# Normalisation and shift applied behind the gate and up products in the second and fourth feed-forward

## What is computed

```python
def rms_norm(x, g):
    y = x * lax.rsqrt(jnp.mean(x * x, axis=-1, keepdims=True) + EPS)
    return y * g
def modulate(h, shift, scale):
    return h * (1.0 + scale[:, None, :]) + shift[:, None, :]
def swiglu(h, w_in, w_out):
    g, u = jnp.split(h @ w_in, 2, axis=-1)
    return (jax.nn.silu(g) * u) @ w_out
h = modulate(rms_norm(x, norm_g[layer, 2]), sh, sc)
x = x + 0.5 * (1.0 + g)[:, None, :] * swiglu(h, ffn_w_in[layer, 1], ffn_w_out[layer, 1])
```

## Time and profile before

| | |
|---|---|
| three runs | 1314.81 us median, 1313.96 to 1315.42 |
| the profiled execution | 1313.54 us, of which 1311.8 us are its span |
| mean granted clock of TensorE | 0.994 of 2.4 GHz |
| busy share of the span | PE 96%, DVE 82%, ACT 48%, POOL 14% |
| `ffn1`, first to last matmul of its units | 254.6 to 444.7 us |
| `ffn3`, the same | 770.2 to 960.3 us |

### The profile page before, as it was taken

One profiled execution on the slowest core, in us unless ns is written; L12 is line 12 of the kernel. 1 busy time (PEld: TensorE's weight loads), 2 busy tenths in 40 slices (PEclk: granted clock), 3 DMA queues, 4 the chain that ended last, 5 costly groups with the idle time before them and its releaser, 6 DMA issues.

```text
span 1311.8 us, 26641 instructions
## 1 busy us (share of the span) xinstructions
PE 1258.3 (96%) x10570; PEld 1228.0 (94%) x10570; DVE 1070.9 (82%) x1668; ACT 629.1 (48%) x990; POOL 189.1 (14%) x204
## 2 busy tenths in 40 slices
PE   2999999999999999999999999999999999999996
PEld 1999999899999889999999999999998989999996
DVE  6998978898888777988878778999978588895674
ACT  3543344544344556553346653434354675455453
POOL 5598800000000000000001000000001014530000
PEclk8999999999999999999999999999999999999999
DMA  9998887389888369988953389887655598555461
GB/s 365 385 338 308 297 312 270 131 324 333 310 304 290 120 203 360 334 293 307 310 205 106 115 250 337 296 304 255 222 182 174 113 185 179 171 163 178 175 196 49
DMA packets 110924, 319.73 MB, mean 244 GB/s; under 512 B 24096, under 2 KB 35808, under 8 KB 110560
## 3 DMA queue, kind: packets, MB, share of 16 engines
q1 hardware_dynamic: 110816, 318.23, 72.8%
HBM read 313.18 MB, written 5.01 MB: 243 GB/s over the span
## 4 chain that ended last, share of the span: by engine, by line
PE 88%; DVE 7%; ACT 3%; issue 1%; DMA 1%; SPq 0%; ACTq 0%; DVEq 0%
PE tiles L375 18%; PE tiles L377 18%; PE tiles L376 18%; PE acc L375 8%; PE acc L377 8%; PE acc L376 8%; PE nrm L551 2%; DVE w_lo L367 2%; PE tiles L577 1%; DVE arena L1468 1%; PE tiles L579 1%; PE tiles L594 1%; ACT w_hi L363 1%; DMA x<-in_x_t 1%; DVE arena L1423 1%
## 5 line engine op out<-in xcount | busy, mean ns | idle before, releaser
L363 ACT CAST w_hi<-land 128x1024 fp32r<-128x1024 f32 x391 | 408.4, 1047 | 457.8 <-PE tiles L377 292.1
L367 DVE TENSOR_TENSOR w_lo<-land,w_hi 128x1024 fp32r<-128x1024 f32 x391 | 486.3, 1251 | 146.0 <-ACT w_hi L363 144.7
L375 PE MATMUL tiles<-x_hi,w_hi 128*128 128x256 f32 x1384 | 393.5, 284 | 0.8 <-DVE arena L1868 0.5
L376 PE MATMUL tiles<-x_lo,w_hi 128*128 128x256 f32 x1384 | 391.6, 283 | 0.0
L377 PE MATMUL tiles<-x_hi,w_lo 128*128 128x256 f32 x1384 | 391.6, 283 | 0.0
L375 PEld LDWEIGHTS tiles<-x_hi,w_hi 128*128 128x128 f32 x1384 | 265.5, 192 | 3.0 <-issue 1.0
L376 PEld LDWEIGHTS tiles<-x_lo,w_hi 128*128 128x128 f32 x1384 | 265.6, 192 | 0.1
L377 PEld LDWEIGHTS tiles<-x_hi,w_lo 128*128 128x128 f32 x1384 | 265.6, 192 | 0.0
L1423 DVE SCALAR_TENSOR_TENSOR arena<-arena 128x1024 f32<-128x1024 f32 x184 | 227.3, 1239 | 11.7 <-ACT arena L1157 8.3
L375 PE MATMUL acc<-h_hi,w_hi 128*128 128x256 f32 x704 | 199.3, 283 | 0.0
L376 PE MATMUL acc<-h_lo,w_hi 128*128 128x256 f32 x704 | 199.2, 283 | 0.0
(11 more groups left out here) (338 smaller groups left out, 1599.7 us busy)
## 6 DMA issues: line engine op xcount, KB each, us to landing
land<-in_stream SPq DMA_DIRECT2D x391, 512.0 KB, 4.5
arena<-in_gstream SPq DMA_DIRECT2D x184, 512.0 KB, 6.5
w_dram<-arena SPq DMA_DIRECT2D x3, 512.0 KB, 6.3
arena<-w_dram SPq DMA_DIRECT2D x6, 256.0 KB, 9.6
arena<-in_c_rows SPq DMA_DIRECT2D x2, 512.0 KB, 5.1
x<-in_x_t SPq DMA_DIRECT2D x1, 1024.0 KB, 10.1
arena<-in_ssm_bn SPq DMA_DIRECT2D x1, 1024.0 KB, 8.2
u_dram<-arena SPq DMA_DIRECT2D x1, 1024.0 KB, 5.3
```

Of the source, the lines that this page charges most:

```text
L363: nc.scalar.copy(w_hi[:, u % RING], land[:, u % LAND]).then_inc(hi_done, 1)
L367: nc.vector.tensor_tensor(w_lo[:, u % RING], land[:, u % LAND], w_hi[:, u % RING].bitcast(F32), ALU.subtract).then_inc(lo_done, 1)
L375: nc.tensor.matmul(outs, lh, rh, start=first, stop=False, **kw)
L376: nc.tensor.matmul(outs, lh, rl, start=False, stop=False, **kw)
```

## The change

In `ffn1` and `ffn3` only (`LATE`), the products with `w_in` are taken of x times (1 + scale) times the norm's gain, without 1/rms; 1/rms (`rx_late`) multiplies gate and up results. The shift is two equal columns more (columns 256 and 257) in the moving operand `xs_hi`, `xs_lo`, so the product of weights and shift comes as a column of each result. `tiles`, `nrm` and `av_bank` become four banks of one tensor `quad`, of which gate and up of one hidden tile take one each. The order of units becomes gate j, output j-2, up j. `keep_busy` goes at these two places; the squares are summed in pairs on VectorE and then by four matmuls in place of eight.

```diff
+            def late_unit(bank, u, i):
+                pe.wait_ge(lo_done, i * 12 + (u + 1))
+                m = products(pe, quad[:, bank, 0:T + 2],
+                             [(*w_tile(u, k * P, P), xs_hi[:, k], xs_lo[:, k]) for k in range(KT)])
+                m.then_inc(used, 1)
+            def ffn_late(f, stage):                                   # TensorE
...
+                first_units(base, [quad[:, b, 0:T + 2] for b in range(3)], xs_hi, xs_lo, KT * stage)
+                for k in range(0, KT, 2):
+                    pe.wait_ge(sq_pair, 4 * e + k // 2 + 1)
+                    m = nc.tensor.matmul(late_sum, ones, t_buf[:, k], start=(k == 0), stop=(k == KT - 2))
+                m.then_inc(nrm_done, 1)
+                late_unit(3, base + 3, 0)
...
+                            pe.wait_ge(silu_done, i * 4 + (FFN_TILES * f + j - 1))
+                            late_unit(2 * (j % 2), g_unit(f, j), i)
+                            out_unit(f, j - 2, o_unit(f, j - 2), i, 4)
+                            pe.wait_ge(freed["d"], i * 4 + (nd + j - 1))
+                            late_unit(2 * (j % 2) + 1, u_unit(f, j), i)
...
-            sum_squares(2)
-            keep_busy(7)
-            ffn(1, 2)
+            ffn_late(1, 2)
...
+            def late_rows(stage, n, ready, unit, before=None):        # ScalarE
+                nc.scalar.activation(eps_root, con("eps", 1), ACT.Sqrt)
+                for k in range(KT):
+                    ready(k)
+                    nc.scalar.activation(x_hi[:, k], x[:, k], ACT.Identity,
+                                         scale=coef[:, stage, k:k + 1]).then_inc(xh_done, 1)
+                for k in range(KT):
+                    nc.scalar.square(t_buf[:, k], x[:, k]).then_inc(sq_done, 1)
+                split_hi(act, unit)
...
+                nc.scalar.activation(rx_late, late_sum, ACT.Sqrt, bias=con("eps", 1), scale=1.0 / D).then_inc(rt_done, 1)
+                nc.scalar.activation(eps_root, con("eps", 1), ACT.Silu)
+            def ffn_late(f):                                          # ScalarE, one round
...
+                            split_hi(act, g_unit(f, j), i)
+                            late_shifts(f, j - 2, i, 4)   # copies the two shift values out of PSUM
+                            late_silu(f, j - 2, i, 4)     # silu(gate + shift), waits for scaled_done
+                            split_hi(act, o_unit(f, j - 2), i)
+                            late_hi(f, j - 2, i, 4)       # h_hi, waits for late_hidden
+                            split_hi(act, u_unit(f, j), i)
...
+            def late_scale(f, j, i, per):                             # VectorE
+                V.tensor_tensor(gate_up[:, j % 2], quad[:, b:b + 2, 0:T], rx_late.unsqueeze(1).to_broadcast([P, 2, T]),
+                                ALU.mult).then_inc(scaled_done, 1)
+            def late_hidden(f, j, i, per):
+                V.scalar_tensor_tensor(out=gate_up[:, j % 2, 1], in0=gate_up[:, j % 2, 1],
+                                       scalar=shift_s[:, j % 2, 1:2], in1=gate_up[:, j % 2, 0],
+                                       op0=ALU.add, op1=ALU.mult).then_inc(freed["d"], 1)
+            def late_lo(f, j, i, per):
+                V.tensor_tensor(h_lo[:, j % 2], gate_up[:, j % 2, 1], h_hi[:, j % 2].bitcast(F32),
+                                ALU.subtract).then_inc(h_done, 1)
...
+                for k in range(0, KT, 2):
+                    dve.wait_ge(sq_done, KT * n + k + 2)
+                    V.tensor_tensor(t_buf[:, k], t_buf[:, k], t_buf[:, k + 1], ALU.add).then_inc(sq_pair, 1)
+                split_lo(dve, unit)
+                dve.wait_ge(rt_done, n + 1)
+                link(V.reciprocal(rx_late, rx_late))
...
                             for s in range(3):
                                 split_lo(dve, u + s, i)
+                                if late and s == 0:
+                                    late_scale(f, j - 2, i, 4)
+                                if late and s == 1:
+                                    late_hidden(f, j - 2, i, 4)
+                                if late and s == 2:
+                                    late_lo(f, j - 2, i, 4)
...
+            norm_coef(2)
+            late_shift(2, 0)
+            split_lo(dve, UNIT["ffn1"] + 1)
             for k in range(KT):
                 wait_tile(dve, TILE["pool"] + k)
                 update(k, tiles[:, k % 2, 0:T], 1, freed["d"])
-            split_lo(dve, UNIT["ffn1"] + 1)
-            norm_coef(2)
```

More of the change, by code:

```diff
@@ L129, in att2_tile, with g_unit, u_unit, o_unit @@
     return TILE["att2+zm"] + 2 * g
-def g_unit(base, j):
-    return base + (2 * j if j < 2 else 3 * j - 1)
-def o_unit(base, j):
-    return base + (65 if j == FFN_TILES - 1 else 3 * j + 4)
+LATE = (1, 3)
+LATE_STAGE = {1: 2, 3: 6}
+def g_unit(f, j):
+    return FFN_BASE[f] + (2 * j if j < 2 else 3 * j - (2 if f in LATE else 1))
+def u_unit(f, j):
+    return FFN_BASE[f] + (2 * j + 1 if j < 2 else 3 * j)
+def o_unit(f, j):
+    if f in LATE:
+        return FFN_BASE[f] + (3 * j + 5 if j < FFN_TILES - 2 else 44 + j)
+    return FFN_BASE[f] + (65 if j == FFN_TILES - 1 else 3 * j + 4)
+def rows_before(stage):
+    return KT * sum(n not in LATE_STAGE.values() for n in range(stage))
 def build_program(nc, stream, gstream, c_rows_d, k_tab_d, vecs_d, cons_d, mask2_d, band_d, xin, pos_d, ssm_bw, ssm_bn, ssm_c, out):
@@ L638, in out_unit @@
                     m = products(pe, yT[n], [(*w_tile(u, n * P, P), h_hi[:, j % 2], h_lo[:, j % 2])],
-                                 start=(j == 0 and per == 0 and n % 2 == 0),
+                                 start=(j == 0 and n % 2 == 0),
                                  stop=(j == FFN_TILES - 1 and per == 0), skip_group_check=True)
@@ new lines, in late_hi @@
+            def late_hi(f, j, i, per):
+                nd = OWNER[:TILE[f"ffn{f}"]].count("d")
+                act.wait_ge(freed["d"], i * per + (nd + j + 1))
+                act.wait_ge(used, i * 3 * per + (FFN_BASE[f] + 3 * j))
+                nc.scalar.copy(h_hi[:, j % 2], gate_up[:, j % 2, 1]).then_inc(late_hh, 1)
+            def ffn_late(f):
+                base = FFN_BASE[f]
+                j0 = 2
+                for part, (reps, _) in enumerate(SEGMENTS[f]):
+                    with act.Fori(0, reps) as i:
+                        for m in range(4):
+                            j = j0 + m
+                            split_hi(act, g_unit(f, j), i)
[4 more added lines that the diff above has]
+                            split_hi(act, u_unit(f, j), i)
+                    j0 += 4 * reps
+                split_hi(act, base + 64)
+                late_shifts(f, FFN_TILES - 2, 0, 0)
+                late_silu(f, FFN_TILES - 2, 0, 0)
+                late_hi(f, FFN_TILES - 2, 0, 0)
+                late_shifts(f, FFN_TILES - 1, 0, 0, 0, 1)
+                late_silu(f, FFN_TILES - 1, 0, 0)
+                split_hi(act, base + 65)
+                late_shifts(f, FFN_TILES - 1, 0, 0, 1, 1)
+                late_hi(f, FFN_TILES - 1, 0, 0)
@@ L1430, in hidden @@
             def hidden(f, j, i, per):
-                base, nd = FFN_BASE[f], OWNER[:TILE[f"ffn{f}"]].count("d")
-                J = FFN_TILES * f + j
+                nd = OWNER[:TILE[f"ffn{f}"]].count("d")
+                J, plain = FFN_TILES * f + j, FFN_TILES * sum(n not in LATE for n in range(f)) + j
                 dve.wait_ge(silu_done, i * per + (J + 1))
@@ new lines, in late_rows @@
+            def late_rows(stage, n, e, unit):
+                for k in range(KT):
+                    dve.wait_ge(xh_done, KT * stage + k + 1)
+                    V.scalar_tensor_tensor(out=x_lo[:, k], in0=x[:, k], scalar=coef[:, stage, k:k + 1],
+                                           in1=x_hi[:, k].bitcast(F32), op0=ALU.mult,
+                                           op1=ALU.subtract).then_inc(xl_done, 1)
+                for k in range(0, KT, 2):
[4 more added lines that the diff above has]
+                link(V.reciprocal(rx_late, rx_late))
@@ L1533, in ffn @@
             def ffn(f, stage, pre, gate_col, ahead_units, next_stage):
-                base, b = FFN_BASE[f], G_FFN[f]
-                for s in range(pre, 5):
-                    split_lo(dve, base + s)
-                hidden(f, 0, 0, 0)
+                base, b, late = FFN_BASE[f], G_FFN[f], f in LATE
+                if not late:
+                    for s in range(pre, 5):
+                        split_lo(dve, base + s)
+                    hidden(f, 0, 0, 0)
                 b += G_FIRST[f]
@@ L1560, in ffn @@
                                     out_part(5 * (part - 1) + OUT_AT.index(3 * m + s))
-                            hidden(f, j - 1, i, 4)
+                            if not late:
+                                hidden(f, j - 1, i, 4)
                             if f == 2:
@@ L1568, in ffn @@
                 blocks[0] = b
-                split_lo(dve, o_unit(base, 21))
+                if late:
```

(14 more changed lines are left out.)

133 lines of the change are left out of this document (88 added, 45 removed).

## The result

| | before | after |
|---|---|---|
| runs side by side | 1314.89 us median (1313.96 to 1315.42) | 1345.93 us median (1344.23 to 1346.73) |
| ratio | | 1.0234, 95% interval 1.0222 to 1.0246 |
| the profiled execution, its span | 1313.54, 1311.8 us | 1346.24, 1344.4 us |

The change makes the kernel 31.0 us slower. Where the time goes is read from four marks, which divide each execution into five stretches: the first matmul of each sum of squares that stands in both kernels (L551 before, L573 after; the one at 15 us is left aside), which is where a stage hands over to the next.

A forecast was written before the change was run, and what follows sets the result against it. TensorE was taken as the bound, 88% of the last-ending chain. Terms -7.4 (starts), +10.5 (first stalls), +9.5 (ffn1), +16.3 (ffn3) sum to +28.9 on 1313.54, giving 1342.4; as a median 1343.7 us, range 1328 to 1352.

The forecast's parts named there:

- The round: In late rounds of ffn1 and ffn3, two VectorE-ScalarE hand-overs make a round 9.01 us against TensorE's 8.67.
- The first stalls: At the start of ffn1 and ffn3, TensorE idles 2.55 us, then 2.7 us again; +10.5 us in all.
- Rival 4: At both starts, two pauses of 2.6 us make the clock fall to 1.2 GHz: +3 to +8, some 1349; chance 0.05.
- Ahead of `ffn1`: Before ffn1's rounds, first units start without the root: 5.6 us gained, 2.9 after squares and columns.
- the last tile: At the end of each late feed-forward, the last tile comes late: 0.7 us in ffn1, 0.8 in ffn3.
- `ffn3`'s rounds: In ffn3, hand-overs plus out_part and power_part beside the rounds; with 0.8 for the last tile, +16.3 us.
- The 1334 at the low end: Whole kernel with silu and late_hi at their lower bounds: 10 us less than the forecast.
- Rivals 1 to 3: The first of these: hand-overs in late rounds are quicker, a round stays under 8.67 us; +16, 1331 us; chance 0.12.
- rival 2: In both late feed-forwards TensorE keeps a lead, so the 7.4 us gain remains: 1307 us; chance 0.07, 0.05 of it faster.
- Rival 3: In gate and up products the two columns cost more than in proportion, 13 ns a matmul: about 1350 us; chance 0.05.

The follow-up runs named there:

- Both together: The changed kernel with both splits (output and up unit) moved ahead in ScalarE's order and gate unit 2's halves made ahead of the root: 1306.99 us.
- The first gate unit's halves: The changed kernel with w_hi and w_lo of gate unit 2 made ahead of the wait for root and reciprocal: 1342.57 us.
- both splits ahead: The changed kernel with ScalarE's split of the output unit ahead of silu and that of the up unit ahead of late_hi: 1310.99 us.

## Why the prediction was right

1343.7 us was predicted and 1345.93 measured; by the profiled executions +28.9 and +32.7.

**The round** was the largest term and holds. Predicted from one `w_lo` of a gate unit to the next, with the idle time ahead of the output unit's `w_lo`: 9.01 and 1.6 us; measured 9.06 outside the loop and 1.57. (By the prediction's own steps the idle time is 3.34 - 1.83 = 1.51; its 1.6 does not follow from them.) Ahead of the up unit's: 0.37 and 0.28 (0.36 in the loop). The durations taken from neighbours were scale 0.69 (measured 0.68), silu from SBUF 0.50 (0.51), `late_hidden` 0.48 (0.48), `late_hi` 0.40 (0.41). That the mechanism is this one, moving one split shows: -33.1 us.

**Too small by 2.0 us:** the twelve rounds of `ffn1` that are a loop take 0.13 and the others 0.05 more than 9.01. The term that was too small is the 0.03 us taken for every hand-over between engines: it holds from ScalarE's split to VectorE's `w_lo`, but scale to silu took 0.09 to 0.10 in every round read, and `late_hidden` to `late_hi` took 0.11 in the loop. No row showed it before, when rounds went at TensorE's pace.

**The first stalls** were 2.55 and 2.7. In `ffn1` 2.59 and 2.52. In `ffn3` 2.65 and 1.00: the second is short only because the gate unit before it ran at the lower clock. Products of 258 columns, timeline of TensorE after:

```profile
792.58 0.42 PE L397 MATMUL quad<-xs_hi,w_hi 128*128 128x258 f32 x1
...
795.16 0.42 PE L397 MATMUL quad<-xs_hi,w_hi 128*128 128x258 f32 x1
```

Twelve products in 2.58 us are 0.215 each: the 1.2 GHz level. **Rival 4 came true in part**, and what it said of the fall being partly under the round too: TensorE would have stood for h in any case. The granted clock is 0.50 in four stretches of the changed kernel: the one of these products, and at the start of `ffn1`, inside `ffn3` and in a stage that was not touched:

```profile
269.80:273.20 3.40, 3.21 (x15) 3.24 (x16) 3.40 (x7) 0.00 (x0) 0.00 (x0) 0.50 0.80 270
874.00:877.40 3.40, 3.40 (x18) 3.40 (x18) 2.71 (x5) 1.19 (x2) 0.00 (x0) 0.50 0.89 340
1201.70:1205.00 3.30, 3.30 (x66) 3.30 (x63) 3.30 (x6) 0.38 (x1) 0.00 (x0) 0.50 0.48 164
```

The pauses of TensorE just ahead of the last two:

```profile
873.38 0.35 PE L397 MATMUL acc<-h_hi,w_hi 128*128 128x256 f32 x1 [2.24 <-DVE h_lo L1584]
1200.54 0.33 PE L1055 MATMUL quad<-arena 64*64 64x64 f32 x2 [2.17 <-DVE arena L2110]
```

So it doesn't take the two pauses of the rival. In `ffn1` the clock falls at the second, in `ffn3` already at the first. In the 14 traces, start-up and the last 20 us aside, there are 23 falls, and each starts within 1.6 us of the end of a pause of 2.0 to 2.7 us, none behind a shorter one. Another 11 pauses of that length are followed by no fall, so the same pause can go either way: of 2.17 us at 1200.54 here with a fall, of 2.16 us at the same line in the kernel with both changes ("Both together") without. The price of the falls at the starts is near nothing, not the 3 to 8 us of the rival: in `ffn1` the slow time lies behind the second stall (an output and the up unit) and the silus come 10.20 and 10.21 us apart, as in the kernel without that fall (10.21 and 10.21, "The first gate unit's halves"); in `ffn3` 9.05 and 9.06 in both. The Trainium skill (TensorE: Matmul & The Clock Gate, A second HAM failure mode: psum-queue depth-cycling) tells of a clock that falls and rises with small idle times between groups; the trace agrees only for pauses of 2 us and more. `ffn1`'s rounds from 298 us on, with a short stop of TensorE in each, are granted 1.00.

**Ahead of `ffn1`** I had first units directly behind the last band matmul. They wait for the last update of x:

```profile
247.24 0.38 PE L812 MATMUL quad<-arena 128*128 128x128 f32 x2
248.25 0.36 PE L599 MATMUL quad<-xs_hi,w_hi 128*128 128x258 f32 x1 [0.62 <-DVE x L1653]
```

The first units use the banks that the updates read (`wait_bank` ahead of `first_units`), a wait that I had not followed: 0.6 us.

**Behind both feed-forwards** the next sum of squares comes 0.9 us later after the last output product than before: 1.13 us of wait, 0.23 at both places of the kernel before. Timeline of ScalarE after:

```profile
453.88 0.41 ACT L1160 CAST h_hi<-arena 128x256 fp32r<-128x256 f32 x1 [2.09 <-DVE arena L1577]
454.19 2.95 ACT L385 CAST w_hi<-land 128x1024 fp32r<-128x1024 f32 x3
457.16 1.28 ACT L1102 ACT_TABLE_LOAD   x1
```

`late_hi` of the last tile waits 2.09 us with three splits and the table load queued behind it. I had costed the last tile up to TensorE's output unit (0.7 and 0.8; measured 0.77 and 0.86) and not what stands behind it in ScalarE's queue. In the kernel with both splits ahead the wait is 0.74 us.

**`ffn3`'s rounds** were laid out at 188.9 us for twenty (20 x 8.67 + 15.5) and took 190.6.

**The rest:** +0.8, not looked for: a wait for the transfer of `ssm_bw` (0.7 us, none before) and later waits of attention products. **What I left out altogether** is TensorE's pace, -2.7 us in the two untouched stretches. The misses add to 0.6 + 2.0 + 2 x 0.9 + 1.7 + 0.8 - 2.7 = 4.2, near the 3.8 by which the sum was short. That the last one takes 2.7 off the others is luck: without it the sum would have been short by 6.5. The 1334 at the low end of the prediction's own bounds doesn't follow from its terms either: silu and `late_hi` at their lower bounds take 0.15 off a round, some 6 us in 38 rounds, not 10.

**Rivals 1 to 3.** The round was not under 8.67, so 1 and 2 are out in this form; with two splits moved, rival 2's condition (TensorE keeps a lead) is met from the second or third round on. Rival 3 is out by the run without columns: two columns cost 0.8 to 1.3 ns a product, not 13.

## What to carry to other kernels

When two engines hand over to each other inside a round, write down what stands in each queue right behind each wait: here a split that VectorE needed soon stood behind a silu that waited, and so was on the chain with its full 1.05 us; moving it ahead gave 33 us back. A bridge removed at a stage's start pays only if the work it hid is short enough for what is now in front of it. And before a gain of half a per cent is put down to an algorithm, run the old kernel with its buffers at the new addresses.

## What the runs showed of the hardware

- **The place of the moving operand acts on TensorE's pace**, by 1 to 3%: 0.1200 us a product of 256 columns at the old places and 64 bytes further, 0.1187 to 0.1189 at 128, 0.1167 to 0.1179 with the operand 16, 144 or 256 bytes further. Over the kernel the moves gave 7.9 to 13 us. No duration in the profile shows it (each matmul row reads 0.28 us); only the distance of starts does. It is not the only thing that acts: at the same 144 bytes products with a stood at 0.1173 in one kernel and 0.1186 in another.
- **The clock falls behind pauses of TensorE of 2.0 to 2.7 us**, one is enough, and not behind each: the traces have 23 falls and 11 such pauses without one. At the lower level the distance of products of 258 columns is 258/1.2 = 215 ns, with nothing on top; at the upper one 12 to 13 ns come on top of 258/2.4 = 107.5. The Trainium skill (TensorE: Matmul & The Clock Gate, Back-to-back issue gap) has N/1.2 and N/2.4 + 2.5 ns for the two, for a matmul by itself: the trace agrees with the first and not with the second.
- **One hand-over takes longer in a loop than written out:** `late_hidden` to `late_hi` 0.11 against 0.03 us, and with it the round 9.14 against 9.06. The other, scale to silu, takes 0.09 to 0.10 in both.
